# A hybrid decoder step on one core: stick-breaking attention with the sample attention inside its head loop

## The chip, the cores and the metric

The kernel runs on one NeuronCore of a Trainium2 chip (trn2). The metric is the device time of one execution in microseconds (us), lower is better. TensorE (PE) multiplies, VectorE (DVE) and ScalarE (ACT) do elementwise work, GpSimd (POOL) builds masks and issues some of the DMAs, SyncE (SP) issues the weight loads.

## The reference, cut to what matters

Two layers are applied to 512 prompt tokens and 8 sample tokens. The change lies in the mixer of layer 1, in its stick-breaking attention, and in how that hands over to the output projection:

```python
    def block(args):
        qblk, b = args
        qpos = offset + b * qb + jnp.arange(qb)
        z = jnp.einsum('bqhd,bkhd->bhqk', qblk, k) * scale + bias
        mask = key_idx[None, :] < qpos[:, None]
        log_1mb = jnp.where(mask, jax.nn.log_sigmoid(-z), 0.0)
        acc = lax.cumsum(log_1mb, axis=3, reverse=True) - log_1mb
        wts = jnp.where(mask, jnp.exp(jax.nn.log_sigmoid(z) + acc), 0.0)
        return jnp.einsum('bhqk,bkhd->bqhd', wts, v)
```

There are 8 heads of 64 elements. The prompt attends to itself (512 keys, strictly earlier ones). Each of the 8 sample tokens attends to 256 cached keys, two pages of 128 found through a page table. Beside the attention stands an RG-LRU group; the projection `w_out` takes both. K and V rows are outputs too.

## The kernel before, in words

All activations lie transposed, features on partitions, 520 tokens in the free dimension. Every matrix product of the big layers is three passes at line 1766 (high and low parts of weight and input); those of the stick-breaking part are plain fp32.

The core's engines run programs written in a fixed order and meet only at semaphores. In the stage `mix_o`, `project_o` computes the tiles Q, K, V (`prO[OQ..]`, `prO[OK..]`, `prO[OV..]`) and the RG-LRU. Then:

- `rows_o`: PE turns V (4 blocks) and K (4 blocks) into rows, and the sample rows of Q, K, V (`rowS`) and of the state (`rowX`). DVE or ACT copies them out of PSUM.
- `stick`: a loop over `h`. The scores of a head are four blocks of 512, 384, 256 and 128 columns (`SCORE`), 1280 in all, for only half of the square is needed. ACT reads them three times (Relu, Relu of the negative, Abs) into `skX`, `skY`, `skL`, and takes Exp and Ln. DVE adds, multiplies the diagonal blocks with the mask `before` (line 1607), sums later blocks (`skR`), and adds to `skY`. PE sums over later keys with `after` and `ones` (lines 2164, 2166) one iteration later. DVE adds that sum to `skY` (1614), ACT takes Exp (1029), POOL masks the diagonal blocks of the weights (652), and PE multiplies with V (2180) two iterations after the scores.
- Each iteration also holds one sample's scores: PE copies the sample's query to all partitions (a product with `ident`), and DVE multiplies it with two pages of keys and reduces (1640, 1641), page by page. When a sample is done, POOL issues two page loads (606).
- `samples_o`, after the loop: softplus, sums over later keys, weights `smW` (1047), products with the V pages (2201), and the high and low parts `oO` of all eight input tiles of the projection (1056, 1674).
- `out_proj`: the projection starts with tile 0.

What sets the order is thus the written order of each engine, and the semaphores `sk_*`, `sm_*`, `page_loaded`.

## Time and profile before

| | |
|---|---|
| median of 3 runs | 2349.86 us (2349.62 to 2350.8) |
| the profiled execution | 2349.4 us, of which the span from first to last instruction is 2347.8 us |
| PE busy | 2242.0 us, 95% of the span |
| DVE busy | 1120.1 us, 48% |
| ACT busy | 788.0 us, 34% |
| POOL busy | 104.3 us, 4% |
| granted TensorE clock, mean | 0.98 of full speed |

The profile gives every instruction a start and a length, and for idle time the instruction that ended it. Times inside the execution are counted from the span's start. The stage that the change touches lies between 1757.5 and 1893.8 us.

### The profile page before, as it was taken

The numbers are of one execution on the slowest core, as the hardware profiler recorded it, in microseconds if no ns is written. First come the engines' busy times: TensorE is split into PE (matmuls) and PEld (weight loads), VectorE is DVE, ScalarE is ACT, GpSimd is POOL, SyncE is SP. The second block draws the span as 40 slices with busy tenths as digits, with TensorE's granted clock in tenths as the row PEclk, the third lists the DMA queues.
The fourth block names the chain that finished last, engine by engine and source line by source line (L and its number), as shares of the span: only waits on it lengthen the run. The fifth ranks groups of instructions, "written<-read, shape, count | busy, mean of one in ns | idle before, by whom it ended". The sixth has DMA issues, their size and how long they took to land.

```text
span 2347.8 us, 43642 instructions
## 1 busy us (share of the span) xinstructions
PE 2242.0 (95%) x17746; PEld 2155.0 (92%) x17746; DVE 1120.1 (48%) x1677; ACT 788.0 (34%) x1068; POOL 104.3 (4%) x178
## 2 busy tenths in 40 slices
PE   8999999998889899999999999999998799999997
PEld 7999999997778699999999999999994389999996
DVE  5444433764346655444334444433667644444332
ACT  5222222352133542222223222223457533222222
POOL 0000001000112200000000000000003200000000
PEclk9999999998899999999999999999998999999998
DMA  4333333321200223333333333232323133333331
GB/s 134 96 89 89 93 92 101 103 81 49 66 1 1 59 73 108 90 89 87 93 90 93 94 90 89 86 99 81 94 87 102 44 92 93 94 89 89 93 90 52
DMA packets 352975, 195.70 MB, mean 83 GB/s; under 512 B 9902, under 2 KB 347978, under 8 KB 352872
## 3 DMA queue, kind: packets, MB, share of 16 engines
q1 hardware_dynamic: 344640, 172.36, 25.6%
q0 software_dynamic: 6064, 19.86, 2.8%
q10 hardware_dynamic: 2176, 2.15, 0.3%
q8 instruction: 68, 1.11, 0.2%
q14 instruction: 27, 0.22, 0.0%
HBM read 186.43 MB, written 8.04 MB: 83 GB/s over the span
## 4 chain that ended last, share of the span: by engine, by line
PE 66%; DVE 4%; ACT 3%; issue 1%; DMA 0%; POOL 0%; POOLq 0%; ACTq 0%; DVEq 0%
PE PS L1766 58%; PE PS L1874 5%; PE PS L2212 1%; PE PS L2180 0%; PE PS L2053 0%; DVE skX L1607 0%; DVE Dm L1440 0%; DVE skX L1622 0%; PE PS L2164 0%; PE PS L2201 0%; ACT skX L1016 0%; ACT skL L1025 0%; ACT skL L1024 0%; ACT skL L1022 0%; ACT skY L1019 0%
## 5 line engine op out<-in xcount | busy, mean ns | idle before, releaser
L1766 PE MATMUL PS<-hh,whi 128*128 128x260 f32 x3600 | 732.5, 285 | 3.1 <-DVE hl L1686 1.8
L1766 PE MATMUL PS<-hh,wlo 128*128 128x260 f32 x3600 | 728.2, 284 | 0.0
L1766 PE MATMUL PS<-hl,whi 128*128 128x260 f32 x3600 | 727.4, 284 | 0.0
L1125 DVE TENSOR_TENSOR wlo<-stage,whi 128x1024 fp32r<-128x1024 f32 x337 | 412.3, 1223 | 451.8 <-ACT whi L687 440.8
L1766 PEld LDWEIGHTS PS<-hh,whi 128*128 128x128 f32 x3600 | 559.5, 190 | 6.0 <-DVE small L1264 1.5
L1766 PEld LDWEIGHTS PS<-hh,wlo 128*128 128x128 f32 x3600 | 558.0, 189 | 0.0
L1766 PEld LDWEIGHTS PS<-hl,whi 128*128 128x128 f32 x3600 | 556.9, 189 | 0.0
L687 ACT ACTIVATE whi<-stage 128x1024 fp32r<-128x1024 f32 x337 | 352.8, 1048 | 253.0 <-PE PS L1766 244.7
L1766 PE MATMUL PS<-act_h,whi 128*128 128x260 f32 x1408 | 283.9, 283 | 0.0
L1766 PE MATMUL PS<-act_h,wlo 128*128 128x260 f32 x1408 | 283.2, 282 | 0.0
L1766 PE MATMUL PS<-act_l,whi 128*128 128x260 f32 x1408 | 282.5, 282 | 0.0
L1162 DVE SCALAR_TENSOR_TENSOR tmp<-PS,rstd 128x520 f32<-128x520 f32 x176 | 123.1, 699 | 280.1 <-PE PS L1766 277.3
L1766 PEld LDWEIGHTS PS<-act_l,whi 128*128 128x128 f32 x1408 | 217.3, 188 | 0.0
L1766 PEld LDWEIGHTS PS<-act_h,whi 128*128 128x128 f32 x1408 | 216.8, 188 | 0.0
L1766 PEld LDWEIGHTS PS<-act_h,wlo 128*128 128x128 f32 x1408 | 216.8, 188 | 0.0
L732 ACT ACTIVATE act_h<-tmp 128x520 f32 (+1 forms) x88 | 56.2, 639 | 413.7 <-DVE tmp L1188 413.7
L729 ACT ACTIVATE tmp<-tmp 128x520 f32<-128x520 f32 x88 | 56.3, 640 | 286.1 <-DVE tmp L1162 286.1
L1191 DVE TENSOR_TENSOR act_l<-tmp,act_h 128x520 f32 (+1 forms) x88 | 61.7, 701 | 79.9 <-ACT act_h L732 79.9
L699 ACT ACTIVATE tmp<-xT 128x520 f32 (+1 forms) x48 | 30.7, 639 | 203.3 <-DVE xT L1202 203.3
L1202 DVE SCALAR_TENSOR_TENSOR xT<-PS,xT 128x520 f32 (+1 forms) x48 | 33.6, 700 | 95.3 <-PE PS L1766 95.3
L1188 DVE TENSOR_TENSOR tmp<-tmp 128x520 f32<-128x520 f32 x88 | 61.6, 700 | 3.0
L1141 DVE SCALAR_TENSOR_TENSOR hl<-xT,prm,hh x40 | 30.4, 760 | 64.2 <-ACT hh L701 64.2
(384 smaller groups left out, 1776.5 us busy)
## 6 DMA issues: line engine op xcount, KB each, us to landing
stage<-in_ffn_w_gate SPq DMA_DIRECT2D x88, 512.0 KB, 3.8
stage<-in_ffn_w_up SPq DMA_DIRECT2D x88, 512.0 KB, 3.8
stage<-in_ffn_w_down SPq DMA_DIRECT2D x64, 512.0 KB, 4.0
stage<-in_w_in_e SPq DMA_DIRECT2D x28, 512.0 KB, 3.7
stage<-in_ffn_w_down SPq DMA_DIRECT2D x32, 384.0 KB, 3.3
stage<-in_w_in_o SPq DMA_DIRECT2D x20, 512.0 KB, 3.8
stage<-in_w_out_e SPq DMA_DIRECT2D x8, 512.0 KB, 4.2
stage<-in_w_out_o SPq DMA_DIRECT2D x8, 512.0 KB, 4.0
```

Source lines behind the costliest of these rows:

```text
L687: act.activation(whi[:, s % SPLIT_SLOTS, :], stage[:, s % STAGE_SLOTS, :], ACT.Copy)\
L699: act.activation(tmp[:, slot, :], tile(xT, m), ACT.Square).then_inc(sq_ready, 1)
L729: act.activation(tmp[:, a, :], tmp[:, a, :], ACT.Silu).then_inc(gate_ready, 1)
L732: act.activation(act_h[:, bass.ds(2 * t + a, 1), :].rearrange("p a b -> p (a b)"), tmp[:, 2 + a, :], ACT.Copy).then_inc(act_hi, 1)
L1125: dve.tensor_tensor(wlo[:, slot, :], stage[:, s % STAGE_SLOTS, :], whi[:, slot, :].bitcast(F32), ALU.subtract).then_inc(lo_ready, 1)
L1141: dve.scalar_tensor_tensor(out=tile(hl, m), in0=tile(xT, m), scalar=prm[:, bass.ds(m + NORM_PRM[k], 1)], in1=tile(hh, m).bitcast(F32), op0 ...
L1162: return dve.scalar_tensor_tensor(out=dst, in0=psum, scalar=scale, in1=two(rstd[:]), op0=ALU.mult, op1=ALU.mult)
L1188: dve.tensor_tensor(tmp[:, 2 + a, :], tmp[:, a, :], tmp[:, 2 + a, :], ALU.mult)\
L1191: dve.tensor_tensor(tile(act_l, 2 * t + a), tmp[:, 2 + a, :], tile(act_h, 2 * t + a).bitcast(F32), ALU.subtract).then_inc(act_lo, 1)
L1202: dve.scalar_tensor_tensor(out=x, in0=psum, scalar=scale, in1=x, op0=ALU.mult, op1=ALU.add)\
L1766: mm = pe.matmul(psum[:, half, :], w, x(k)[:, half * HALF:(half + 1) * HALF], start=first and w is hi and x is rhs_hi, stop=last and w is lo)
L1874: return pe.matmul(out, w, x, start=True, stop=True)
```

## The change

For the prompt's heads:

- The scores of head 0 are computed before V, K and the sample rows are turned; those of head 1 after. In the loop PE does `sums(h)`, `output(h - 1)`, `score(h + 2)`.
- Each diagonal score block gets a second product, `ident` times `hide`, which adds -2^60 where a key is not earlier. The masks on DVE and POOL go.
- ACT reads the scores once (Identity with the bias) into `skZ`. DVE cuts them at 40 (`cut`), ACT takes Exp and Ln, and softplus is the larger of the score and that. The sum over later keys now includes the key itself (`upto` in place of `after`), and DVE subtracts it from the scores in place. The two copies into `skR` are gone; PE reads those blocks from `skX` in products of their own.

For the samples:

- The query rows go to DRAM once (`q_rows`), and POOL loads each to all partitions (`load_q`) in two slots, each load after an earlier sample is done. DVE works on both pages of a sample at once.
- Samples are spread as 0 in iteration 0, then 1 and 2, 3 and 4, 5 and 6, and 7 in iteration 4. Bias, softplus, sums, exponents and weights follow inside iterations 4 to 6. Two samples' products with V pages come before the last head's output, six after.

For the rest: the turned sample and state rows are spread over iterations 0 to 3; the high and low parts of the projection's inputs are made inside the loop; the projection takes the four RG-LRU tiles first.

```diff
+                def load_q(b):
+                    pool.dma_start(qrow[:, b % 2, :], q_rows[b:b + 1, :].to_broadcast([P, WC])).then_inc(q_loaded[b % 2], 16)
...
-                pool.wait_ge(v_rows, NB)
+                pool.wait_ge(v_rows, 1)
+                pool.dma_start(q_rows, rowS[:, 0, :]).then_inc(q_saved, 16)
+                pool.wait_ge(q_saved, 16)
+                load_q(0)
+                load_q(1)
+                pool.wait_ge(v_rows, 1 + NB)
                 save(o["sbv_p"][0, 0].rearrange("(c p) h d -> p c (h d)", p=P), vtok[:])
                 pool.wait_ge(k_rows, NB)
                 save(o["sbk_p"][0, 0].rearrange("(c p) h d -> p c (h d)", p=P), ktok[:])
-                pool.wait_ge(v_rows, NB + 3)
-                save(o["sbk_s"][0, :, 0].rearrange("b h d -> b (h d)"), rowS[:, 1, :])
-                save(o["sbv_s"][0, :, 0].rearrange("b h d -> b (h d)"), rowS[:, 2, :])
-                pool.wait_ge(k_rows, NB + 2)
+                for n in range(TS):
+                    pool.wait_ge(sm_kq, n + 1)
+                    load_pages(n + 4)
+                    if n + 2 < TS:
+                        load_q(n + 2)
...
+                def softplus_parts(h):
+
+                    act.wait_ge(sk_z, h + 1)
+                    if h >= 3:
+                        act.wait_ge(sk_o, h - 2)
+                    act.activation(skZ[:, h % 3, :], banks(0, 3)[:, 0:SCORES], ACT.Identity, bias=sbb[:, 0, h:h + 1])\
+                       .then_inc(sk_read, 1)
+                    act.wait_ge(sk_cut, h + 1)
+                    link(act.activation(skL[:], skL[:], ACT.Exp))
+                    act.activation(skL[:], skL[:], ACT.Ln, bias=1.0).then_inc(sk_ln, 1)
...
-                        act.activation(skX[:, h % 2, :], z, ACT.Relu, bias=sbb[:, 0, h:h + 1])
-                        if h >= 3:
-                            act.wait_ge(sk_o, h - 2)
-                        act.activation(skY[:, h % 3, :], z, ACT.Relu, scale=-1.0, bias=sbb[:, 1, h:h + 1])
-                        if h:
-                            act.wait_ge(sk_added, h)
-                        act.activation(skL[:], z, ACT.Abs, bias=sbb[:, 0, h:h + 1]).then_inc(sk_read, 1)
-                        act.wait_ge(sk_read, h + 1)
-                        link(act.activation(skL[:], skL[:], ACT.Exp, scale=-1.0))
-                        act.activation(skL[:], skL[:], ACT.Ln, bias=1.0).then_inc(sk_ln, 1)
-                    if 1 <= h <= HC:
-                        act.wait_ge(sk_add, h)
-                        a = (h - 1) % 3
-                        act.activation(skY[:, a, :], skY[:, a, :], ACT.Exp, scale=-1.0).then_inc(sk_w, 1)
...
+                act.wait_ge(o_loaded, 96)
+                softplus_parts(0)
+                key_rows()
+                for h in range(HC):
+                    if h + 1 < HC:
+                        softplus_parts(h + 1)
+                    weights(h)
+                    if h >= 1:
+                        output(h - 1)
+                    if h < 4:
+                        row_out(h)
+                    if h < KR:
+                        act.activation(oO[:, OX + h, :], prO[:, OY + h, :], ACT.Copy).then_inc(o_hi, 1)
+                    if h == 4:
+                        sample_softplus()
+                    if h == 6:
+                        sample_weights()
+                output(HC - 1)
+
...
+                def cut(h):
+
+                    dve.wait_ge(sk_read, h + 1)
+                    if h:
+                        dve.wait_ge(sk_sp, h)
+                    dve.tensor_scalar(skL[:], skZ[:, h % 3, :], STICK_CLAMP, None, ALU.min).then_inc(sk_cut, 1)
+
+                def softplus(h):
+
+                    sp = skX[:, h % 2, :]
+                    dve.wait_ge(sk_ln, h + 1)
+                    if h:
+                        dve.wait_ge(sk_acc, h)
+                    link(dve.tensor_tensor(sp, skZ[:, h % 3, :], skL[:], ALU.max))
+                    x1, x2, x3 = (sp[:, at:at + w] for at, w in SCORE[1:])
+                    dve.tensor_tensor(skR[:, 0:P], x1[:, P:2 * P], x2[:, 0:P], ALU.add)
+                    link(dve.tensor_tensor(skR[:, 2 * P:], x2[:, P:], x3, ALU.add))
+                    dve.tensor_tensor(skR[:, P:2 * P], x1[:, 2 * P:], skR[:, 2 * P:], ALU.add).then_inc(sk_sp, 1)
...
-                    dve.tensor_tensor(skY[:, h % 3, :], skY[:, h % 3, :], skL[:], ALU.add).then_inc(sk_added, 1)
-                    dve.wait_ge(sk_added, h + 1)
-                    sample_scores(h)
-                add_later(HC - 1)
+                    if h + 1 < HC:
+                        cut(h + 1)
+                    if 1 <= h <= 4:
+                        for b in range(2 * h - 1, min(2 * h + 1, TS)):
+                            sample_scores(b)
+                    if h == 4:
+                        sample_bias()
+                    elif h == 5:
+                        sample_softplus()
+                    elif h == 6:
+                        sample_exponents()
+                    dve.wait_ge(sk_acc, h + 1)
+                    dve.tensor_tensor(skZ[:, h % 3, :], skZ[:, h % 3, :], banks(3, 3)[:, 0:SCORES], ALU.subtract)\
+                       .then_inc(sk_sub, 1)
...
             def sample_scores(b):

-                dve.wait_ge(sm_q, b + 1)
+                dve.wait_ge(q_loaded[b % 2], 16 * (b // 2 + 1))
                 dve.wait_ge(page_loaded[b % 4], 16 * PAGES * (b // 4 + 1))
-                for p in range(PAGES):
-                    link(dve.tensor_tensor(kq[:], pages[:, b % 4, p, :], banks(7, 1), ALU.mult))
-                    last = dve.tensor_reduce(smS[:, 0, p, b, :], kq[:].rearrange("p (h d) -> p h d", h=HC), AX.X, ALU.add)
-                    if p < PAGES - 1:
-                        link(last)
-                last.then_inc(sm_kq, 1)
-                dve.wait_ge(sm_kq, b + 1)
-
...
+                def score(h):
+
+                    r = slice(h % 2 * HDC, (h % 2 + 1) * HDC)
+                    if h:
+                        pe.wait_ge(sk_read, h)
+                    for n, (at, w) in enumerate(SCORE):
+                        z = banks(0, 3)[:, at:at + w]
+                        pe.matmul(z, prO[r, OK + h // 2, n * P:(n + 1) * P], prO[r, OQ + h // 2, n * P:TP],
+                                  start=True, stop=False)
+                        mm = pe.matmul(z[:, 0:P], ident[:], hide[:], start=False, stop=True)
+                    mm.then_inc(sk_z, 1)
+
...
+                    later = [[(x1[:, 0:P], P), (skR[:, 0:2 * P], 2 * P)], [(x2[:, 0:P], P), (skR[:, 2 * P:], P)], [(x3, P)]]
+                    if h:
+                        pe.wait_ge(sk_sub, h)
+                    pe.wait_ge(sk_sp, h + 1)
+                    for n, (at, w) in enumerate(SCORE):
+                        acc = banks(3, 3)[:, at:at + w]
+                        mm = pe.matmul(acc, upto[:], sp[:, at:at + w], start=True, stop=n == NB - 1)
+                        to = P
+                        for x, size in later[n] if n < NB - 1 else ():
+                            mm = pe.matmul(acc[:, to:to + size], ones[:], x, start=False, stop=to + size == w)
+                            to += size
+                    mm.then_inc(sk_acc, 1)
...
+                score(0)
+                for m in range(KC):
+                    mm = turn(banks(6, 1)[0:TS, m * P:(m + 1) * P], prO[:, OQ + m, TP:TOK], P)
...
+                for c in range(NB):
+                    turned(OV, c, VALUE_BANKS[c])
+                for c in range(NB):
+                    pe.wait_ge(v_rows, 1 + c)
+                    turned(OK, c, KEY_BANKS[c])
+                score(1)
+                pe.wait_ge(k_rows, NB)
+                for h in range(HC):
+                    sums(h)
+                    if h >= 1:
+                        output(h - 1)
+                    if h + 2 < HC:
+                        score(h + 2)
+                    if h < 4:
+                        row(h)
+                    if h == 5:
+                        sample_sums()
+                sample_outputs(0, 2)
+                output(HC - 1)
+                sample_outputs(2, TS)
...
+                    out_proj(s, "out_o0", lambda m: oO[:, OK + m if m < KC else OX + m - KC, :],
+                             lambda m: oO[:, OQ + m if m < KC else OY + m - KC, :],
+                             lambda k: pe.wait_ge(o_lo, O_PARTS + (OD_LO[k - KC] if k >= KC else KC + KR + 1)),
+                             list(range(KC, KC + KR)) + list(range(KC)))
```

On DVE, one whole head of the loop, before (`skX`, `skY`, `skL` as above; `kq` is the product of a page with a query, `before` the mask):

```order
L1614 TENSOR_TENSOR skY<-skY,PS 128x1280 [waits sk_acc,sm_kq]
L1622 TENSOR_TENSOR skX<-skX,skL 128x1280 [waits sk_ln]
L1607 TENSOR_TENSOR skX<-skX,before 128x128 [waits dve_chain]
L1607 TENSOR_TENSOR skX<-skX,before 128x128 x3
L1626 COPY skR<-skX 128x128 [waits dve_chain]
L1627 COPY skR<-skX 128x128
L1628 TENSOR_TENSOR skR<-skX 128x128
L1629 TENSOR_TENSOR skR<-skX,skR 128x256 [waits dve_chain]
L1630 TENSOR_TENSOR skY<-skY,skL 128x1280
L1640 TENSOR_TENSOR kq<-pages,PS 128x512 [waits page_loaded1,sm_q,sk_added]
L1641 TENSOR_REDUCE smS<-kq 128x8 [waits dve_chain]
L1640 TENSOR_TENSOR kq<-pages,PS 128x512 [waits dve_chain]
```

And in the changed kernel, iteration 1, a head with two samples (`tmp` holds the query copies and the products):

```order
L1658 TENSOR_SCALAR skL<-skZ 128x1280 [waits sk_sp,sk_read]
L1718 TENSOR_TENSOR tmp<-pages,tmp 128x2x512 [waits sm_kq,page_loaded1,q_loaded1]
L1719 TENSOR_REDUCE smS<-tmp 128x2x8 [waits dve_chain]
L1718 TENSOR_TENSOR tmp<-pages,tmp 128x2x512 [waits sm_kq,page_loaded2,q_loaded0]
L1719 TENSOR_REDUCE smS<-tmp 128x2x8 [waits dve_chain]
L1699 TENSOR_TENSOR skZ<-skZ,PS 128x1280 [waits sk_acc]
L1666 TENSOR_TENSOR skX<-skZ,skL 128x1280 [waits sk_acc,sk_ln]
L1668 TENSOR_TENSOR skR<-skX 128x128 [waits dve_chain]
L1669 TENSOR_TENSOR skR<-skX 128x128
L1670 TENSOR_TENSOR skR<-skX,skR 128x128 [waits dve_chain]
L1675 TENSOR_TENSOR oO<-prO,oO 128x520 [waits o_hi]
```

Four masks, two copies and one addition of 1280 columns have gone; a tensor-scalar instruction has come; two samples of twice the width now stand between the cut and the subtraction, and wait for query loads.

On POOL's queue, from the last key page of the first four samples, before:

```order
L611 DMA out_rgc_s<-in_state_rg_conv 8x1024
L611 DMA out_sbv_p<-vtok 128x4x512 [waits v_rows]
L611 DMA out_sbk_p<-ktok 128x4x512 [waits k_rows]
L611 DMA out_sbk_s<-rowS 8x512 [waits v_rows]
L611 DMA out_sbv_s<-rowS 8x512
L611 DMA out_rgh_p<-rowX 16x1x32 [waits k_rows]
L611 DMA out_rgh_s<-rowX 8x512
L611 DMA out_rgc_p<-rowX 3x512
L611 DMA out_rgc_s<-rowX 8x512
L603 TENSOR_LOAD ptab [waits sm_kq]
L606 ISA
L606 DMA pages<-in_cache_sb_k 128x512
```

And in the changed kernel:

```order
L641 DMA out_rgc_s<-in_state_rg_conv 8x1024
L664 DMA q_rows<-rowS 8x512 [waits v_rows]
L626 DMA tmp<-q_rows 128x512 [waits q_saved]
L626 DMA tmp<-q_rows 128x512
L641 DMA out_sbv_p<-vtok 128x4x512 [waits v_rows]
L641 DMA out_sbk_p<-ktok 128x4x512 [waits k_rows]
L633 TENSOR_LOAD ptab [waits sm_kq]
L636 ISA
L636 DMA pages<-in_cache_sb_k 128x512
L633 TENSOR_LOAD ptab
L636 ISA
L636 DMA pages<-in_cache_sb_k 128x512
```

A store of the query rows and two loads that read it back now stand ahead of the stores of V and K; the small stores have moved behind the loop's page loads.

On PE, the end of the stage before, from the output of head 6 (`skY` against `vtok`) to the first V pages of the samples:

```order
L2180 MATMUL PS<-skY,vtok 64x512 [waits sk_mask,sk_oc]
L2180 MATMUL PS<-skY,vtok 64x384
L2180 MATMUL PS<-skY,vtok 64x256
L2180 MATMUL PS<-skY,vtok 64x128
L2180 MATMUL PS<-skY,vtok 64x512 [waits sk_mask,sk_oc]
L2180 MATMUL PS<-skY,vtok 64x384
L2180 MATMUL PS<-skY,vtok 64x256
L2180 MATMUL PS<-skY,vtok 64x128
L2191 MATMUL PS<-smS,after 128x64 [waits sk_add,sm_step]
L2193 MATMUL PS<-smS,ones 128x64
L2191 MATMUL PS<-smS,after 128x64
L2201 MATMUL PS<-pages,smW 64x512 [waits page_loaded0,consts,sm_w]
```

And in the changed kernel, from the output of head 6:

```order
L2261 MATMUL PS<-skZ,vtok 64x512 [waits sk_w,sk_oc]
L2261 MATMUL PS<-skZ,vtok 64x384
L2261 MATMUL PS<-skZ,vtok 64x256
L2261 MATMUL PS<-skZ,vtok 64x128
L2309 MATMUL PS<-pages,smW 64x512 [waits page_loaded0,sm_w]
L2309 MATMUL PS<-pages,smW 64x512
L2309 MATMUL PS<-pages,smW 64x512 [waits page_loaded1]
L2309 MATMUL PS<-pages,smW 64x512
L2261 MATMUL PS<-skZ,vtok 64x512 [waits sk_w,sk_oc]
L2261 MATMUL PS<-skZ,vtok 64x384
L2261 MATMUL PS<-skZ,vtok 64x256
L2261 MATMUL PS<-skZ,vtok 64x128
```

The sample sums (`smS` with `after`) no longer stand between the last head and the V pages, and the last output now follows two samples.

## Rows read from the trace of the kernel before

**Rows 1.** The page of the profile, its first line.

```profile
span 2347.8 us, 43642 instructions
```

**Rows 2.** Windows: stretch, length, busy us (instructions) by engine, granted clock, DMA share, GB/s.

```profile
1765.89:1778.37 12.48, 8.07 (x18) 4.17 (x18) 3.42 (x10) 8.96 (x8) 9.37 (x17) 0.71 0.82 282
1778.37:1858.37 80.00, 69.33 (x223) 37.99 (x224) 73.19 (x110) 54.73 (x47) 21.42 (x42) 0.94 0.18 56
1858.37:1893.76 35.39, 24.97 (x63) 9.08 (x63) 4.90 (x11) 6.78 (x26) 7.14 (x14) 0.86 0.23 74
```

**Rows 3.** Timeline, TensorE: start, us, what, count, idle before and its releaser.

```profile
1757.52 7.12 PE L2212 MATMUL PS<-ident,prO 128*128 128x128 f32 x48 [2.77 <-DVE prO L1162]
...
1772.19 4.63 PE L1874 MATMUL PS<-prO 64*128 64x512 f32 x8 [2.87 <-ACT skL L1022]
1778.37 2.08 PE L2164 MATMUL PS<-skX,after 128*128 128x512 f32 x2 [1.55 <-DVE skR L1629]
...
1812.79 1.10 PE L2164 MATMUL PS<-skX,after 128*128 128x512 f32 x2 [0.55 <-DVE skR L1629]
...
1816.98 1.12 PE L1874 MATMUL PS<-rowS,ident 8*128 8x512 f32 x2 [0.50 <-DVE smS L1641]
1818.03 2.37 PE L2180 MATMUL PS<-skY,vtok 128*64 128x512 f32 x8
1820.33 2.42 PE L1874 MATMUL PS<-prO 64*128 64x512 f32 x8
1823.22 1.10 PE L2164 MATMUL PS<-skX,after 128*128 128x512 f32 x2 [0.47 <-DVE skR L1629]
...
1886.50 3.65 PE L2201 MATMUL PS<-pages,smW 128*64 128x512 f32 x8 [0.24 <-DMA pages<-in_cache_sb_v]
...
1893.76 0.93 PE L1766 MATMUL PS<-oO,whi 128*128 128x260 f32 x4 [1.78 <-DVE oO L1674]
```

**Rows 4.** Groups by line and shape, 1745 to 1900: busy us, mean ns, idle before, releasers.

```profile
L1622 DVE TENSOR_TENSOR skX<-skX,skL 128x1280 f32<-128x1280 f32 x8 | 11.9, 1490 | 11.0 <-ACT skL L1025 11.0
L1614 DVE TENSOR_TENSOR skY<-skY,PS 128x1280 f32<-128x1280 f32 x8 | 11.9, 1486 | 3.6 <-PE PS L2164 3.4
...
L1640 DVE TENSOR_TENSOR kq<-pages,PS 128x512 f32<-128x512 f32 x16 | 11.0, 687 | 0.6
L1641 DVE TENSOR_REDUCE smS<-kq 128x8 f32<-128x512 f32 x16 | 11.0, 686 | 0.6
...
L1016 ACT ACTIVATE skX<-PS,sbb 128x1280 f32<-128x1280 f32 x8 | 10.6, 1327 | 12.8 <-PE PS L1874 12.8
...
L1024 ACT ACTIVATE skL<-skL 128x1280 f32<-128x1280 f32 x8 | 10.2, 1270 | 0.3
```

**Rows 5.** Timeline, VectorE, one tensor-scalar instruction.

```profile
1744.60 0.43 DVE L1567 TENSOR_SCALAR tmp<-tmp 128x520 f32<-128x520 f32 x1
```

**Rows 6.** Windows on TensorE's granted clock in four stretches.

```profile
1757.50:1761.00 3.50, 3.48 (x17) 3.48 (x18) 3.35 (x8) 0.00 (x0) 0.43 (x1) 0.51 0.52 154
1788.90:1795.10 6.20, 5.33 (x9) 2.94 (x10) 4.84 (x8) 4.56 (x4) 0.23 (x1) 0.50 0.01 1
1851.80:1854.70 2.90, 0.03 (x1) 0.06 (x1) 2.83 (x9) 0.59 (x1) 1.52 (x4) 1.00 0.25 81
1893.76:1897.40 3.64, 3.64 (x18) 3.64 (x19) 3.64 (x7) 3.64 (x7) 0.00 (x0) 0.55 0.00 0
```

**Rows 7.** Timeline, GpSimd: issues of its DMA queue.

```profile
1772.65 0.53 POOL L611 DMA_DIRECT2D out_rgc_s<-in_state_rg_conv  x1
...
1884.44 0.54 POOL L606 DMA_DIRECT2D pages<-in_cache_sb_v  x1 [0.37 <-issue]
```

**Rows 8.** DMA issues, 1755 to 1900: count, KB each, median us to landing.

```profile
pages<-in_cache_sb_k POOLq DMA_DIRECT2D x16, 256.0 KB, 3.2
...
out_rgc_s<-in_state_rg_conv POOLq DMA_DIRECT2D x1, 32.0 KB, 3.5
out_sbk_s<-rowS POOLq DMA_DIRECT2D x1, 16.0 KB, 6.1
```

325 lines of the change are left out of this document (158 added, 167 removed).

## The prediction

> **What bounds the kernel now.** I read the page first: the span is 2347.8 us [rows 1], the profiled execution 2349.4 us, so 1.6 us lie around the span. Over the whole kernel PE is busy 95%, so only a stage in which PE waits can give much. The windows cut the changed stage in three [rows 2]: 12.48 us from the first scores to the first sum over later keys, 80.00 us of head loop, 35.39 us of tail up to the projection. PE is busy 8.07, 69.33 and 24.97 us of these, and the granted clock is 0.71, 0.94 and 0.86 of full. Ahead of them PE turns V, K and sample rows from 1757.52 on [rows 3]; that makes 136.24 us from 1757.52 to the projection's first product at 1893.76.
>
> The timeline shows the loop's rhythm: sums start at 1812.79 and again at 1823.22, a period of 10.43 us [rows 3]. In it PE works 9.4 us: sums, query copy, output, scores. It waits 0.5 us twice, both times for DVE. DVE is busy 73.19 of the 80.00 us [rows 2], so DVE and PE alternate as the last to finish.
>
> The clock matters too. While the first and second head wait, PE runs at half clock: 0.50 from 1788.90 to 1795.10 [rows 6], and the scores of head 1 take 4.63 us where they later take 2.42 us [rows 3].
>
> **The change, part by part.** I walk the new order with durations of rows.
>
> *Start.* Up to 1757.52 nothing changes. Then PE does `score(0)`. The main part costs 2.42 us at full clock and 4.63 at half [rows 3]. PE has just waited 2.77 us, and the same stretch ran at 0.50 before, from 1757.5 to 1761.0 [rows 6]; I keep that. The four `hide` products add 512 columns to 1280, so 0.4 of 2.3 us, some 0.9 us at full clock. The scores end near 1762.5. Identity takes 1.33 us [rows 4]. The cut is a tensor-scalar; 520 columns took 0.43 us [rows 5], and by the ratio of 1280 to 520 columns its upper bound at that rate is 1.06; I take 0.9 and keep 1.49 (the two-input form, [rows 4]) as the bound above, 0.43 below. It stands behind the copies of the query rows and of V block 0, so it ends near 1765.4. Exp and Ln at 1.27 each [rows 4] end at 1768.0. Softplus is one maximum (1.49) and three 128-column additions. The 512- and 1280-column forms (0.687 and 1.49, [rows 4]) give 0.15 + 0.00105 per column, so 0.29 each, 2.3 in all: 1770.3. PE meanwhile turns 36 blocks at 0.15 (7.1 us for 48, [rows 3]), and does `score(1)` (3.2): 1770.6. So the first sums start at 1770.6 in place of 1778.37: **7.8 us earlier**.
>
> *Loop, PE's share.* Sums: 2048 columns as before, 3.65. Output 2.3, scores 2.3 + 0.9 = 3.2, together 9.1; the query copy (1.05) is gone. Four rows of turns add 0.6 in iterations 0 to 3.
>
> *Loop, DVE's share.* Cut 0.9, subtraction 1.49, softplus 2.3: 4.6 us per head. A sample is a product and a reduction over 1024 columns, 1.22 each by the same line: 2.5 us (bounds 2.2 and twice 1.37 = 2.75, from the 512-column rows). A head with two samples costs DVE 9.6, plus 0.7 for a low part, and the cut first waits for ACT's Identity, 1.3 to 2 us after the sums of the head before could start: a period of **12.0 us**. So in iterations 1 to 3 DVE, not PE, sets the pace. In iterations without samples PE does (9.1 to 9.7).
>
> *The queries.* POOL reaches the new store after the page issues, at 1773.2 [rows 7]. Like the small store at 3.5 us [rows 8] it lands near 1777.2; the load behind it is 256 KB written like a page (3.2 us, [rows 8]), so query 0 is there at 1780.4. DVE could start sample 0 at 1778.1: 2.4 us late, all of it on DVE's path. The query of sample 2 is issued behind two page issues after sample 0 and lands near 1787.9, 1 us late. Later ones hide under the 5 us of the neighbouring sample and the 4.6 us of the head. Behind DVE's wait stand the subtraction and softplus of that head, and PE waits for these.
>
> Starts of sums: 1770.6, 1778.1, 1794.2, 1806.0, 1818.5, 1829.3, 1839.4, 1846.9, end 1850.6. (In iterations 2 and 4 the sums run at half clock after PE's wait of 6.4 and 2.7 us; what it costs is 1.0 us in all, for DVE has samples to do then.) First start to last end: 80.0 us, **as long as before**. The gain of removed masks and the shorter chain is spent on samples packed two to a head and on queries.
>
> *Tail.* From the end of the last sums: output(6) 2.3, two samples, output(7) 2.3, six samples. Two samples' V products took 3.65 us at full clock [rows 3], so eight cost 14.6, by the walk with 1.75 each 14.0. Their weights are ready: softplus, sums and exponents lie inside iterations 4 to 6, beside PE's 9.1 us. The last four V groups are issued when the first four are used, 1.8 us each on POOL. Before, the last issue came at 1884.44 and the product that needed it started with the group of 1886.50 [rows 3, 7]; now POOL issues from 1854.6, the last lands near 1864, and it is needed at 1867. Then `smO` (0.8), four small products (1.05), and the projection starts at 1871.1 with the RG-LRU tiles, whose parts are ready; their 2.9 us cover the last copies of the sample columns, which before delayed it 1.8 us [rows 3]. 1850.6 to 1871.1 is 20.5 us in place of 35.39: **14.9 us less**.
>
> *Behind it.* The projection's first 3.64 us ran at 0.55 of the clock after the waits [rows 6], which lost 0.45 of 3.64, 1.6 us. In the walk PE is busy up to 1.9 us before and waits only 0.8 in one piece, so I credit the 1.6 us.
>
> Sum: 7.8 + 0 + 14.9 + 1.6 = 24.3. Against the profiled execution of 2349.4: **2325.1 us**. The median of the runs shown is 0.5 higher, so this holds for it within that.
>
> **A rule of the skill against it.** First the row: DVE's tensor-scalar ran at 0.43 us for 520 columns where a two-input instruction of 512 took 0.687 [rows 4, 5], so the cut uses a faster form. The Trainium skill, page "SBUF — State Buffer", section "Who interferes with whom", says that such a form locks GpSimd out of a shared port, and that a DMA issued from GpSimd then starves because its descriptors can't be written. By that rule a cut could hold a page or query issue for its 0.9 us, and two query loads lie on the path. By the row alone the sum is 2325.1; by the rule it is 0.9 to 1.8 us more, up to 2326.9. The trace before has no instruction of this kind and length beside a DMA issue, so it doesn't decide.
>
> **The rivals.**
>
> 1. *Forecast, 0.60:* 2321 to 2330.
> 2. *Queries on time and samples cheaper, 0.15.* With query 0 here 2 us earlier sums 2 starts 2 us earlier: 2323, still case 1. With samples at their lower 2.2 us, 3 us less: 2320. The 1.0 us of clock and a cut of 0.5 us take it to 2318. For it: the product before read its query from PSUM, now from SBUF, and both pages go in one instruction. Against it: 5 of DVE's 9.6 us would have to beat the column line.
> 3. *Queries late, 0.18.* Small stores beside big ones landed after 6.1 us [rows 8]. With query 0 at 1785 and each load 3 us slower, sums 2 starts 7.6 us later, the rest holds: 2333. With cut and samples at their upper bounds, 3 more: 2336. For it: page loads fill the DMA engines then, 282 GB/s and a share of 0.82 [rows 2].
> 4. *Slower than before, 0.03: TensorE stays at half clock through the loop.* PE's waits of 2 to 6 us could keep it there. Eight heads at 18.2 us, less the two score sets (6.3 each) and the output (4.6) that fall away at the ends, plus 4.8 of turned rows, are some 131 us from 1770.6; the tail twice as long (41) brings the projection to 1942, 48 later than before: 2397. A us at half clock costs at most 0.5, so it decides when some 49 of the stage's 113 us run so. Against it: in the old loop the clock stayed at 1.00 even through a wait of 2.9 us [rows 6], and at half clock PE has no waits left, after which it rose each time.
> 5. *Does not do what it says, 0.04 with no change.* The period is not fixed (12 us in three heads), as in the forecast; a full loss of 24 us would need each query load to take some 12 us instead of 3.2 and query 0 at 1788, by the same walk. Nothing in [rows 8] is near.
>
> **The numbers.** A measurement here tells 0.2% (4.7 us) from no change. Faster: cases 1, 2 and 3, 0.93. Same: case 5, 0.04. Slower: case 4, 0.03. Range: from case 2's lower end with a margin to case 3's, 2316 to 2337; what lies outside is case 4, 5 and the ends of 2 and 3, under 2 in 10.
>
> **What the new profile would show.** Right: first scores at 1757.5, first sums near 1770.6; periods near 12 us in iterations 1 to 3 with PE waiting for DVE's softplus, near 9.5 after iteration 4; DVE waiting for a query's load once or twice, 1 to 2.5 us each; the last sums' end 20 us before the projection, with no wait for pages over 1 us; the clock at 0.50 in short stretches only. Wrong would be: waits for queries in every pair of samples; a cut of 1.4 us; the projection waiting for its last four tiles; or a loop well under 77 us, which would mean that I overprice the samples.

## The result, and the profile after

The changed kernel took 2330.68 us (median of 4 runs, 2328.81 to 2331.24), the kernel before on the same chip 2349.95 us (4 runs, 2349.62 to 2350.8): a ratio of 0.9916, 95% interval 0.9899 to 0.9933, so **19.3 us faster**. The prediction said 2325.1 us, 24.3 less, range 2316 to 2337. Medians leave out two executions in a disturbed state: one of the kernel "tail undone" below, 7648.7 us, and one of the kernel before beside it, 2763.5 us.

The page's first line and the windows of the three parts, which answer to [rows 1, 2]. The cuts are the same: first product of the stage, first sums, end of the last sums, the projection's first product.

```profile
span 2328.8 us, 43715 instructions
```

```profile
1758.29:1776.19 17.90, 17.90 (x69) 11.00 (x69) 9.02 (x17) 5.81 (x7) 8.47 (x23) 0.71 0.50 151
1776.19:1857.55 81.36, 75.86 (x313) 45.62 (x311) 55.69 (x70) 47.23 (x64) 17.62 (x32) 0.96 0.33 105
1857.55:1876.54 18.99, 17.51 (x58) 6.63 (x57) 3.46 (x4) 3.08 (x4) 4.34 (x8) 1.00 0.37 111
```

The stage takes 118.25 us where it took 136.24: 18.0 less. It starts at another time in every run (1753.8 to 1758.9 in the runs of this study, from work ahead of the edit), so below parts are compared by their length. The projection's first products now run at full clock, as predicted: from the first of them to the end it is 454.0 us before and 452.3 now. The stage began 0.8 us later, so the span is 19.0 us shorter.

| part | before | predicted | measured |
|---|---|---|---|
| first product to first sums | 20.85 | 13.1 | 17.90 |
| first sums to end of last sums | 80.0 | 80.0 | 81.36 |
| to the projection | 35.39 | 20.5 | 18.99 |

PE was busy 69.33 of the loop's 80.00 us before [rows 2], now 75.86 of 81.36; DVE fell from 73.19 to 55.69. Where the start went, in the timeline of TensorE (start, us, what, count, idle before):

```profile
1758.29 2.03 PE L2232 MATMUL PS<-prO 64*128 64x512 f32 x2 [2.78 <-DVE prO L1214]
1760.25 0.80 PE L2234 MATMUL PS<-hide,ident 128*128 128x128 f32 x2
...
1766.46 5.29 PE L2322 MATMUL PS<-ident,prO 128*8 128x128 f32 x36
1771.67 1.12 PE L2232 MATMUL PS<-prO 64*128 64x512 f32 x2
1772.73 0.49 PE L2234 MATMUL PS<-hide,ident 128*128 128x128 f32 x2
...
1775.86 0.49 PE L2234 MATMUL PS<-hide,ident 128*128 128x128 f32 x2
1776.19 1.02 PE L2247 MATMUL PS<-skX,upto 128*128 128x512 f32 x2
```

(The profile lists each of these fp32 products as two instructions, so x8 is four products.) `score(0)` takes 8.17 us, from 1758.29 to 1766.46, and `score(1)`, at full clock, 4.52 us. I had written 5.0 and 3.2. The windows of the same stretch give the clock in the third column from the end:

```profile
1759.30:1766.46 7.16, 7.16 (x16) 3.50 (x15) 1.92 (x4) 0.00 (x0) 2.88 (x13) 0.50 0.24 72
1766.46:1769.00 2.54, 2.54 (x15) 2.29 (x14) 1.27 (x2) 1.33 (x1) 1.65 (x3) 0.58 0.54 127
1769.00:1771.60 2.60, 2.60 (x24) 2.35 (x22) 2.60 (x5) 1.70 (x2) 1.81 (x3) 1.00 0.78 216
```

PE was never idle there, and still the granted clock was at 0.50, the level of 1.2 GHz, through all of `score(0)` (0.54 in its first us) and for the first 2.1 us of the turns. Before, the turns stood here and had the clock back after 3.5 us [rows 6].

### The profile page after: what moved, and what is told of

Its sections match the earlier page's. It is cut to its first block, busy times and chain, and to the rows that moved or that the text cites. A ratio compares the mean times of both kernels' runs of the same rounds, so it can differ in the third digit from the quotient of the medians.

```text
span 2328.8 us, 43715 instructions
## 1 busy us (share of the span) xinstructions
PE 2242.3 (96%) x17826; PEld 2159.1 (93%) x17826; DVE 1095.4 (47%) x1620; ACT 769.0 (33%) x1055; POOL 94.1 (4%) x157
## 3 DMA queue, kind: packets, MB, share of 16 engines
q10 hardware_dynamic: 2176, 2.15, 0.3%
q8 instruction: 68, 1.11, 0.2%
## 4 chain that ended last, share of the span: by engine, by line
PE 67%; DVE 3%; ACT 2%; issue 1%; DMA 0%; POOLq 0%; POOL 0%; ACTq 0%; DVEq 0%
PE PS L1848 58%; PE PS L1956 5%; PE PS L2322 1%; PE PS L2232 1%; PE PS L2247 1%; PE PS L2234 0%; PE PS L2250 0%; PE PS L2261 0%; PE PS L2135 0%; DVE Dm L1492 0%; PE PS L2309 0%; DVE skX L1666 0%; DVE tmp L1718 0%; PE PS L1863 0%; DVE dif L1449 0%
```

## The experiments

For every kernel the table gives its median and its ratio to the kernel before (95% interval), and from its trace the lengths of the three parts and of the whole stage. "Masks of 64 rows" has two runs, the others four. An interval is 4 us wide on either side, and the kernel before took 2348.7 to 2351.0 us on the chips used, so differences of a few us between these kernels rest on the parts. Code that is the same does not repeat exactly: the unchanged start took 17.79 to 17.94 us in five kernels and 19.09 in one, where the clock came back later; the wait for the query of sample 2 was 1.53, 1.91 and 2.24 us in three kernels with the same loop up to there; and one period of the loop swings by 1.7 us (told under the query order).

| kernel | us | ratio | start | loop | tail | stage |
|---|---|---|---|---|---|---|
| changed | 2330.7 | 0.9916 (0.9899-0.9933) | 17.90 | 81.36 | 18.99 | 118.25 |
| no masks | 2326.7 | 0.9896 (0.988-0.9913) | 13.04 | 80.97 | 18.84 | 112.85 |
| masks batched | 2325.5 | 0.9901 (0.9884-0.9917) | 15.50 | 80.19 | 18.80 | 114.49 |
| masks of 64 rows | 2325.9 | 0.9895 (0.9875-0.9915) | 15.39 | 78.09 | 19.23 | 112.71 |
| turns first | 2328.1 | 0.9911 (0.9894-0.9927) | 15.98 | 83.14 | 18.91 | 118.03 |
| query first | 2325.4 | 0.9894 (0.9878-0.9911) | 17.79 | 78.21 | 18.63 | 114.63 |
| query first, no product | 2323.3 | 0.9891 (0.9873-0.9908) | 17.90 | 73.78 | 18.24 | 109.92 |
| query first, early Identity | 2323.9 | 0.9897 (0.9879-0.9914) | 19.09 | 74.63 | 18.83 | 112.55 |
| tail undone | 2338.3 | 0.996 (0.9944-0.9977) | 17.94 | 79.42 | 29.03 | 126.39 |
| projection in natural order | 2330.7 | 0.9916 (0.9899-0.9933) | 17.94 | 80.31 | 19.98 | 118.23 |
| three edits | 2324.2 | 0.9901 (0.9883-0.9919) | 14.76 | 78.36 | 18.73 | 111.85 |
| four edits | 2321.7 | 0.9879 (0.9862-0.9895) | 14.53 | 75.63 | 18.96 | 109.12 |
| four edits, store first | 2319.5 | 0.9867 (0.985-0.9883) | 14.85 | 71.90 | 19.03 | 105.78 |

### What a mask product costs: three kernels

Without the masks (the scores then hold pairs that should be hidden):

```diff
-                        mm = pe.matmul(z[:, 0:P], ident[:], hide[:], start=False, stop=True)
```

> Leaves out the four mask products per head (the scores then also hold pairs that should be hidden, so the output is not the reference's; the work on DVE and ACT stays the same). In the changed kernel a set of scores takes 4.5 us at full clock, where the set without mask took 2.42 us [rows 3]. Theory A: a mask product costs more than its 128 columns, because the 64-row scores and the 128-row mask products alternate; without them a set takes 2.4 us, score(0) 4.6 us at half clock, and the stage gets shorter by about 3.5 us at its start and by 2.1 us in each head that PE paces (iterations 0, 5 and 6; 1 to 4 are paced by DVE with two samples): 7 to 10 us in all, about 2322. Rival B: a mask product costs its 128 columns (0.23 us), 0.9 us per set; then a set still takes some 3.6 us without them, and the whole gain is 3 to 4 us, about 2327.

Batched, so that PE changes between 64 and 128 contracted rows twice per set instead of eight times:

```diff
+                    masked(NB - 1, True, False)
+                    main(NB - 1, False, True)
+                    for n in range(NB - 1):
+                        main(n, True, False)
+                    for n in range(NB - 1):
+                        mm = masked(n, False, True)
```

> The same products in another order: the mask of the last block first, then the four score products, then the other three masks, so PE changes between 64 and 128 rows twice per set instead of eight times. Theory A (the change of rows, or the weight load it exposes, is the cost): a set takes about 3.4 us at full clock instead of 4.5, sums(0) starts some 2 us earlier, and the time falls by 3 to 5 us, to about 2327. Rival B (a 128-column fp32 product with its own weight load takes 0.42 us wherever it stands): a set stays at 4.3 to 4.5 us and the time is unchanged within 1 us.

And with masks over the scores' own 64 rows, in the old alternation (half of the pairs are hidden):

```diff
-                        mm = pe.matmul(z[:, 0:P], ident[:], hide[:], start=False, stop=True)
+                        mm = pe.matmul(z[:, 0:P], ident[r, :], hide[r, :], start=False, stop=True)
```

> The mask products contract over the same 64 rows as the scores (a half of identity and mask, so only a half of the pairs is hidden and the output is not the reference's); the order alternates as in the changed kernel and the columns are the same. Theory A: what made a mask product cost 0.5 us instead of 0.26 is the change between 64 and 128 contracted rows; then a set takes 3.4 to 3.6 us, like the batched order, and the start is 1 to 3 us shorter. Rival B: it is the change of operand or of weights between score and mask; then a set still takes 4.5 us and nothing changes.

`score(1)` in the three timelines, no masks first, then batched, then 64 rows:

```profile
1768.63 2.42 PE L2232 MATMUL PS<-prO 64*128 64x512 f32 x8
```

```profile
1768.61 2.42 PE L2232 MATMUL PS<-prO 64*128 64x128 f32 x8
1770.96 0.94 PE L2237 MATMUL PS<-hide,ident 128*128 128x128 f32 x6
1771.73 1.02 PE L2257 MATMUL PS<-skX,upto 128*128 128x512 f32 x2
```

```profile
1767.88 1.12 PE L2232 MATMUL PS<-prO 64*128 64x512 f32 x2
1768.84 0.38 PE L2234 MATMUL PS<-hide,ident 64*128 64x128 f32 x2
1769.06 0.81 PE L2232 MATMUL PS<-prO 64*128 64x384 f32 x2
...
1771.12 1.12 PE L2247 MATMUL PS<-skX,upto 128*128 128x512 f32 x2
```

The set takes 2.4 us without masks, 3.44 batched (with 0.32 for the one mask ahead), 3.24 with 64 rows, 4.52 as changed. So four masks of 128 columns are worth 0.22 us each, my 0.9 per set; what I missed is the alternation. The changed set has eight changes of the number of rows, with the one from the turns ahead of it; the batched and the 64-row set have two each. Six changes fewer save 1.08 and 1.28 us, so a change costs some 0.2 us (0.18 and 0.21). Operand and weights alternate in the 64-row kernel too, so rival B of that run falls, as does rival B of the other two: it is the rows. Whether the change itself takes the time, or a weight load of 128 rows that shows only in this alternation, is not separated.

Theory A was right on the set and too high on the whole for the first kernel (2326.7, not 2322; 5.4 us of the stage, not 7 to 10): its loop is no shorter. The total is close to the 2327 of rival B, but its set of 3.6 us is not what was measured. The timeline of VectorE in the kernel without masks says why:

```profile
1781.78 1.23 DVE L1718 TENSOR_TENSOR tmp<-pages,tmp 128x1024 f32<-128x1024 f32 x1 [2.35 <-DMA tmp<-q_rows]
...
1791.55 1.23 DVE L1718 TENSOR_TENSOR tmp<-pages,tmp 128x1024 f32<-128x1024 f32 x1 [3.56 <-DMA tmp<-q_rows]
```

The loop came 4.9 us earlier to samples whose queries did not: sums(2) start 38.9 us after the stage's first product, in the changed kernel 40.1.

### The clock at the start

```diff
-                score(0)
                 for m in range(KC):
                     mm = turn(banks(6, 1)[0:TS, m * P:(m + 1) * P], prO[:, OQ + m, TP:TOK], P)
                 mm.then_inc(row_t, 1)
                 for c in range(NB):
                     turned(OV, c, VALUE_BANKS[c])
+                score(0)
```

> Query rows and the four V turns first, then score(0), then the K turns and score(1); DVE copies the four V blocks before the first cut. Theory A: the scores with their 64 rows kept TensorE at half clock for 10 us at the start of the changed kernel (0.50 through all of score(0), 8.2 us, while PE was never idle), and turns bring it back in some 3.5 us as they did before [rows 6]. Then the turns take 3 us, score(0) 4.5 to 5 us instead of 8.2, and sums(0) start about 13 to 15 us after the stage's start instead of 17.9: 3 to 4 us less, about 2327. Rival B: the clock returns a fixed time after PE's wait ahead of the stage, whatever PE does; then score(0) still runs mostly at half clock, now later, and the time is the same or 1 to 2 us longer.

The windows of this kernel over the turns and over `score(0)`:

```profile
1756.20:1760.00 3.80, 3.80 (x20) 3.44 (x20) 3.66 (x9) 0.00 (x0) 0.77 (x1) 0.56 0.48 142
1760.06:1764.50 4.44, 4.44 (x17) 2.32 (x17) 2.09 (x4) 0.00 (x0) 2.17 (x14) 1.00 0.00 0
```

The 20 turns run at half clock and the scores behind them at full. Rival B falls: a fixed time after the wait would have put `score(0)` at half clock here too. The kernel without masks says the same from the other side, in its windows over scores, first turns and later turns:

```profile
1758.90:1763.40 4.50, 4.50 (x8) 2.44 (x8) 2.84 (x7) 0.00 (x0) 1.21 (x4) 0.51 0.40 120
1763.43:1766.00 2.57, 2.57 (x15) 2.32 (x15) 1.34 (x3) 1.33 (x1) 1.56 (x9) 0.54 0.01 3
1766.00:1768.60 2.60, 2.60 (x25) 2.39 (x23) 2.58 (x5) 1.74 (x2) 1.23 (x3) 1.00 0.08 28
```

Its scores took 4.5 us instead of 8.2, and again the clock rose some 2.4 us into the turns (2.1 in the changed kernel). In all nine traces with scores first it rose 1.9 to 4.8 us into the turns, and never within the scores; the start with no edit in it that took 19.09 us is the one with 4.8. In the four traces with turns first it rose 2.8 to 3.4 us after the first turn, and `score(0)` ran at 1.00. The time expected (3 to 4 us less) did not come: the start is 1.9 us shorter (PE now waits 1.06 us for the softplus, DVE having copied four V blocks first), and the loop gives it back, since DVE waits 2.40 us for the query of sample 2 instead of 1.53. In the stage's length theory A failed, in its mechanism it held.

### The queries

```diff
                 for n in range(TS):
                     pool.wait_ge(sm_kq, n + 1)
-                    load_pages(n + 4)
                     if n + 2 < TS:
                         load_q(n + 2)
+                    load_pages(n + 4)
```

> POOL issues the next query load ahead of the two page loads of the same turn, not behind them. Theory: the changed kernel waited for a query once, 1.53 us ahead of sample 2, and that wait was on DVE's path in a head that DVE paces; without it sums(2) start 1.5 us earlier and the time is 1.0 to 1.5 us less, about 2329. Rival: the wait is hidden (sums(2) waited 2.68 us for the softplus, but the page of the sample would be late next), and nothing changes.

The wait is gone, and sums(2) start 1.6 us earlier (38.49 instead of 40.09 us from the stage's start), as expected. The loop is 3.15 us shorter, though. The other 1.7 us are in sums(4), at the same wait of 1.19 us in both traces, the changed kernel first:

```profile
1823.12 1.95 PE L2247 MATMUL PS<-skX,upto 128*128 128x512 f32 x2 [1.19 <-DVE skR L1670]
```

```profile
1820.43 1.10 PE L2247 MATMUL PS<-skX,upto 128*128 128x512 f32 x2 [1.19 <-DVE skR L1670]
```

The first ran at half clock, the second at full. The period behind it is 12.14 and 10.46 us. This is the swing of 1.7 us between executions of the same code: the kernel with the projection's order undone, whose loop has no edit, had 10.46 as well. It is no gain of the edit.

### What sets the period of 12.2 us

```diff
-                link(dve.tensor_tensor(kq, pages[:, b % 4], q, ALU.mult))
-                dve.tensor_reduce(smS[:, 0, :, b, :], kq.rearrange("p a (h d) -> p a h d", h=HC), AX.X, ALU.add)\
+                dve.tensor_reduce(smS[:, 0, :, b, :], pages[:, b % 4].rearrange("p a (h d) -> p a h d", h=HC), AX.X, ALU.add)\
```

> The query load ahead of the page loads (as in the experiment on the query order), and DVE's product of pages and query left out: only the reduction over the page remains, so a sample costs DVE 1.22 instead of 2.44 us, and the samples' scores are not the reference's. Theory A: in heads with two samples DVE's samples lie on the cycle that sets the period of 12.2 us (cut, samples, subtraction on DVE, then weights, output and Identity on ACT, then the next cut); with 2.4 us less, PE's own 11.0 us set the period, iterations 1 to 4 lose 1.2 to 1.6 us each, and the time is 4 to 5 us below the experiment on the query order alone, about 2321. Rival B: PE's work alone is the bound of the whole loop, its waits of 1 to 3 us are accidents: no change against that experiment.

```diff
                     if h + 1 < HC:
-                        softplus_parts(h + 1)
-                    weights(h)
+                        logs(h + 1)
                     if h >= 1:
                         output(h - 1)
+                    if h + 2 < HC:
+                        identity(h + 2)
+                    weights(h)
```

(DVE's low parts also come one iteration later)

> The query load ahead of the page loads, and ACT's order turned: Identity of head h+2 comes ahead of the weights of head h, right behind the output's copy; DVE makes the low parts one iteration later, so that they don't wait for ACT. No work is added or taken away on any engine. Theory A: in heads with two samples no engine is full; the period of 12.2 us is a cycle through both: cut 0.83, samples 4.9, subtraction 1.5 on DVE, weights 1.3, copies 1.6, Identity 1.3 on ACT, and back to the cut. With Identity out of this cycle, the period falls to PE's 11.0 us (DVE's own work is 10.3), iterations 1 to 4 lose 1.2 to 1.6 us each: 4 to 5 us below the experiment on the query order alone, about 2321. Rival B (my prediction's words): DVE's own work sets the pace at 12 us; then an order that leaves its work as it is changes nothing.

Both bring the periods of iterations 1 to 4 down: 10.82, 10.82, 10.83, 10.38 without the product; 11.71, 10.90, 10.82, 10.39 with the early Identity; 12.18, 12.59, 12.18, 10.46 with the query order alone. The second kernel does the same work as the third in another order, so the rival falls that DVE's own work is the pace. The 12.59 is not the chain's: PE waits for nothing ahead of sums(3) there, it ran at half clock behind its wait of 1.19 us ahead of sums(2). With that wait short or gone the clock does not fall, and this is some 1.7 us of either gain. Against the query order alone the loops are 4.4 and 3.6 us shorter, the medians only 2.1 and 1.5 us, which the intervals do not resolve; the early Identity's start was 1.3 us longer by the late clock just told of, not by its order (PE waits for nothing there).

The chain can be read in the changed kernel's timelines, ScalarE and then VectorE, from sums(3) at 1810.94 to sums(4) at 1823.12:

```profile
1811.14 0.59 ACT L1038 ACTIVATE rowS<-PS 8x512 f32<-8x512 f32 x1 [1.34 <-PE PS L2322]
1811.64 0.62 ACT L1080 ACTIVATE oO<-prO 128x520 fp32r<-128x520 f32 x1
1812.16 1.30 ACT L1047 ACTIVATE skZ<-PS,sbb 128x1280 f32<-128x1280 f32 x1
```

```profile
1813.50 0.83 DVE L1658 TENSOR_SCALAR skL<-skZ 128x1280 f32<-128x1280 f32 x1 [0.51 <-ACT skZ L1047]
1814.24 1.22 DVE L1718 TENSOR_TENSOR tmp<-pages,tmp 128x1024 f32<-128x1024 f32 x1
...
1819.24 1.48 DVE L1699 TENSOR_TENSOR skZ<-skZ,PS 128x1280 f32<-128x1280 f32 x1
...
1822.68 0.29 DVE L1670 TENSOR_TENSOR skR<-skX,skR 128x128 f32<-128x128 f32 x1
```

PE's row turns end as sums(3) start; ACT copies the row, makes an RG-LRU high part and only then runs Identity, 2.56 us in all up to the cut; cut, two samples, subtraction and softplus take DVE the other 9.6 us. That is 12.18. In the kernel with the early Identity PE is the pace: 3.65 of sums, 2.3, 4.5 and 0.45 are 10.9.

### The tail and the projection

The samples' chain moved back behind the loop:

```diff
-                sample_outputs(0, 2)
                 output(HC - 1)
-                sample_outputs(2, TS)
+                sample_sums()
+                sample_outputs(0, TS)
```

(with bias, softplus and exponents on DVE and the two ACT parts behind their loops in the same way)

> Only the tail part is taken back: bias, softplus, sums and exponents of the samples and their weights run after the loop, as in the kernel before, with output(7) ahead of all eight samples' V products; everything else is as in the changed kernel. Theory: this move is what made the tail short. From the last sums to the projection it took 18.9 us in the changed kernel; undone, output(7) (2.3 us at half clock) is followed by waits of 2 to 2.5 us for each step of the samples' chain, as in [rows 3] before the products, so the tail gets some 8 to 10 us longer, and the projection's first products fall back to half clock: 2339 to 2342 us. Rival: the V pages are the limit of the tail (the changed kernel waited for them twice, 0.36 and 0.34 us); then the delay is mostly absorbed by the wait for pages, and the loss is under 4 us.

The tail is 10.0 us longer, the median 7.6, so this part holds; the timeline of TensorE has the waits:

```profile
1856.82 2.37 PE L2256 MATMUL PS<-skZ,vtok 128*64 128x512 f32 x8 [1.20 <-ACT prO L1062]
...
1863.18 13.26 PE L2302 MATMUL PS<-pages,smW 128*64 128x512 f32 x24 [3.19 <-ACT smW L1100]
1876.87 3.65 PE L2302 MATMUL PS<-pages,smW 128*64 128x512 f32 x8 [0.43 <-DMA pages<-in_cache_sb_v]
```

Pages are waited for by 0.43 us only, so they are not the limit. One expectation failed: the clock fell in this tail, but it was back before the projection. The window has 0.68, and the later ones 1.00:

```profile
1862.00:1872.00 10.00, 8.82 (x15) 2.68 (x16) 0.00 (x0) 1.13 (x12) 2.21 (x4) 0.68 0.22 62
```

What keeps it at the projection is the next kernel's subject.

```diff
-                             lambda k: pe.wait_ge(o_lo, O_PARTS + (OD_LO[k - KC] if k >= KC else KC + KR + 1)),
-                             list(range(KC, KC + KR)) + list(range(KC)))
+                             lambda k: pe.wait_ge(o_lo, O_PARTS + KC + KR + 1))
```

> The projection takes its eight tiles in their natural order, so its first product waits for the last low part (the sample columns), as in the kernel before; all else is as in the changed kernel, where the RG-LRU tiles come first and the first product starts 118.25 us after the stage's start, with the clock at 1.00. The last low part there ends 0.8 us behind the first product. Theory (my prediction's): the tile order hides the last copies and keeps the clock, so without it the first product comes 0.8 us later and the projection's first 3.6 us run at half clock again (0.55 before), 1.6 us more: 2.4 us in all, about 2333. Rival: the clock is kept by the busy tail alone, not by the order; then only the 0.8 us are lost and the clock stays at 1.00.

Its timeline at the projection, and the windows behind:

```profile
1872.14 1.06 PE L1956 MATMUL PS<-of_sample,smO 64*128 64x8 f32 x8 [0.78 <-DVE smO L1752]
1874.06 0.72 PE L1848 MATMUL PS<-oO,whi 128*128 128x260 f32 x4 [0.87 <-DVE oO L1758]
```

```profile
1875.06:1876.06 1.00, 1.00 (x7) 1.00 (x6) 1.00 (x1) 0.00 (x0) 0.00 (x0) 0.56 0.00 0
1876.06:1877.06 1.00, 1.00 (x7) 1.00 (x6) 0.06 (x1) 0.00 (x0) 0.00 (x0) 0.50 0.00 0
...
1878.06:1879.06 1.00, 1.00 (x8) 1.00 (x8) 0.00 (x0) 0.00 (x0) 0.00 (x0) 0.73 1.03 306
```

A wait of 0.87 us behind the 0.78 for `smO` and its four short products is enough: the clock is at or near half for 3.5 us, which loses 1.7: in the first 20 us of the projection TensorE ran 154 instructions here and 168 in the changed kernel, 0.12 us each. With the 1.0 us of the longer tail that is 2.7, where 2.4 was expected, and the rival falls. The median (2330.71) does not show it. Its profiled execution took 2331.0 and the changed kernel's 2330.7; its loop was 1.05 us shorter by the swing above, its stage began 2.5 us earlier, and the rest lies within the spread between runs.

### Versions that gather the edits

The three edits are the batched masks, the turns first and the query ahead of the pages; the fourth is the early Identity, its diff above.

> Three edits together: mask products batched, turns of queries and V ahead of score(0), and the query load ahead of the page loads. In single runs the stage (first instruction to the projection's first product) took 114.5 us with the masks batched, 118.0 with the turns first (sums(0) came 1.9 us earlier, but sums(2) did not, for they stood behind the query load) and 114.6 with the query first, against 118.25 in the changed kernel. Theory: the three add up, since the start's gain is no longer lost to a late query: sums(0) 14.5 us after the stage's start, loop 78 us, tail 18.6 us, 111 us in all, so 7 us less than the changed kernel, about 2323. Rival: the period of 12.2 us in heads with two samples swallows PE's cheaper scores, and the sum is only 3 to 4 us less.

> All four edits: masks batched, turns of queries and V first, query load ahead of the page loads, and ACT's Identity ahead of the weights with DVE's low parts one iteration later. Stage lengths so far: changed kernel 118.25, the first three edits together 111.85 (loop 78.4), the query order and the early Identity together 112.55 (loop 74.6, PE the pace at 10.8). Theory: with the cycle broken and the set of scores at 3.5 us, the period is PE's 9.9 or DVE's 10.3; loop 71 to 73 us, start 15 to 16, tail 18.8: stage 105 to 108, about 2319 to 2320, 11 us less than the changed kernel. Rival: the queries set the first two heads (sums(2) no earlier than 36.5 us after the stage's start) and the clock falls to half more often because PE waits more; stage 109 to 110, no better than the single steps by more than 3 us.

The last one also moves the store of the query rows ahead of the pages:

```diff
-                for g in range(4):
-                    load_pages(g)
-                save(o["rgc_s"][0, :, 0:CW - 2, :], i["state_rg_conv"][0, :, 1:CW - 1, :])
                 pool.wait_ge(v_rows, 1)
                 pool.dma_start(q_rows, rowS[:, 0, :]).then_inc(q_saved, 16)
+                for g in range(2):
+                    load_pages(g)
                 pool.wait_ge(q_saved, 16)
                 load_q(0)
                 load_q(1)
```

(groups 2 and 3 and the save follow)

> The same four edits, and POOL stores the query rows ahead of the first page loads and loads queries 0 and 1 after two page groups instead of four. Theory: in the changed kernel query 0 landed some 23 us after the stage's start, just when DVE wanted it; in the three edits together DVE waited 0.8 and 1.3 us for queries. With the store early no sample waits except perhaps sample 2, sums(2) start 1 to 2 us earlier than in the version with four edits, and the stage is 1 to 2 us shorter. Rival: DVE's own order (sample 0 behind softplus(1)) sets sums(2), and nothing changes.

Three edits: 111.85 us where 111 was expected, start, loop and tail each within 0.4 us. Four edits: 109.1, where the expectation was 105 to 108; its rival held for the first heads (sums(2) at 37.1, DVE waits 0.93 and 2.26 us for queries, and sums(2) run at half clock behind PE's wait of 4.84). Store first removes one of these waits and halves the other; sums(2) start at 35.3 and the clock does not fall:

```profile
1773.39:1845.30 71.91, 66.95 (x311) 43.16 (x311) 55.06 (x70) 45.80 (x64) 18.05 (x33) 1.00 0.41 133
```

The stage is 3.3 us shorter than with four edits, more than the 1 to 2 expected: 2.15 us are PE's shorter wait ahead of sums(2), and 1.5 the stretch at half clock behind it, which falls away. At 2319.5 us (2318.59 to 2319.65) this kernel beats the kernel before and the changed one: its ratio to the kernel before, 0.985 to 0.9883, lies clear of the changed kernel's 0.9899 to 0.9933. From the four edits' 0.9862 to 0.9895 it is not told apart; there only the stage speaks.

## Why the prediction was right in sign and 5.6 us too low

The parts account for 4.7 of it (4.8 and 1.4, less 1.5); 0.8 is the later start of the stage in the profiled execution, which is in no edit.

**Start: forecast 7.8 us less, measured 20.85 - 17.90 = 2.95.** This is the step that failed, by 4.8 us. Two terms of it were mis-sized. The first is the clock: the prediction let it rise at 1761.0 as before ("I keep that") and so had "the scores end near 1762.5"; it rose only when turns followed, so `score(0)` took 8.17 us. The row against it was at hand: in the kernel before, the scores at 1772.19 took 4.63 us with PE busy throughout [rows 3]. The second is the price of the masks: "0.9 us" for the four is right for their columns (0.22 each), with 1.3 us per set missing for the changes between 64 and 128 rows. The turns took 5.2 us, about as written. PE's sum also has a slip: 1762.5, 36 turns at 0.15 and 3.2 end at 1771.1, not 1770.6.

**Loop: forecast 80.0 us, measured 81.36.** Right in size, and partly by luck. The period of 12.0 us for heads with two samples was measured as 12.18 from sums(3) to sums(4), with the parts named there, the wait for Identity among them. The two periods ahead of it are something else: 13.67 has the query wait of 1.53 us in it, and in 12.56 PE did not wait: it is PE's own 10.8 and 1.7 for the half clock behind its wait of 2.68 us. That DVE "sets the pace" is true only with ACT's 2.56 us ahead of it, as the early Identity shows. PE's share was put at 9.1 to 9.7 and is 10.4 to 11.0, by the changes of rows. Against this, sample 0 did not wait for its query (forecast 2.4 us), because the sums came later; of the query waits one was left, 1.53 us ahead of sample 2, where 1 had been forecast. PE waited 2.68 and 1.19 us ahead of sums(2) and sums(4) instead of 6.4 and 2.7, and each time the clock fell for some 3.5 us, which costs 1.7 us each, not "1.0 us in all".

**Tail: forecast 14.9 us less, measured 16.4.** The mechanism held: with the chain put back the tail is 10.0 us longer. Waits for pages came to 0.36 and 0.34 us. The 1.5 us lie in "output(7) 2.3": its eight instructions lie beside those of the samples' V products in the timeline of TensorE, not between them:

```profile
1859.75 2.31 PE L2309 MATMUL PS<-pages,smW 128*64 128x512 f32 x5
1861.47 0.64 PE L2261 MATMUL PS<-skZ,vtok 128*64 128x512 f32 x1
1861.89 0.59 PE L2309 MATMUL PS<-pages,smW 128*64 128x512 f32 x1
1861.95 0.59 PE L2261 MATMUL PS<-skZ,vtok 128*64 128x512 f32 x1
...
1863.61 3.17 PE L2309 MATMUL PS<-pages,smW 128*64 128x512 f32 x7
```

From 1859.75 to 1863.61, 3.86 us, stand nine V instructions and all eight of output(7). Twelve V instructions alone take 5.36 us later in this tail, some 0.43 each, so nine need 3.9 us: the output cost nothing. The waits for pages (0.7) and slightly longer V products took 1.0 us of this back.

**Clock at the projection: forecast 1.6 us, right:** the first 20 us of the projection held 154 instructions before and 168 now, 14 of 0.12 us, so 1.7. But its reason was wrong: not the busy tail keeps the clock, the order of the tiles does: behind the tail with waits of 1.20 and 3.19 us the projection started at full clock too, and behind the unchanged tail in natural order it did not.

**The cut** took 0.84 us, forecast 0.9; a sample 2.44, forecast 2.5; softplus 2.3 as forecast. The rule that the prediction set against its sum, a cut that holds an issue, brought nothing onto the path here: neither query load that mattered was held by a cut. Where an issue did meet one, the trace agrees with the rule (last section).

**The rivals.** Case 3 ("queries late") gave the right interval edge, 2333, for a reason that was not there. Cases 4 and 5 did not come (the walk of case 4 adds up to 133 us, not 131, which changes nothing). No rival named what happened: the clock held down by the kind of products.

## What to carry to other kernels

Price a stretch of TensorE by the kind of its products and not by columns alone: a change between 64 and 128 contracted rows cost some 0.2 us each time, so small products of another height belong in one batch, and after a wait the 128-row work belongs ahead of the 64-row work. Follow the cycle through all engines before naming one as the pace: an instruction that another engine waits for goes ahead of copies that nobody waits for. And ask of an earlier start which DMA it will now meet: of the 4.9 and 1.9 us by which two edits (no masks, turns first) brought sums(0) forward, sums(2) kept 1.2 and 1.1, for they stood behind query loads.
